# Two of the four low quarters of one weight slab moved from VectorE to GpSimd

## The chip, the cores and the metric

The kernel runs on one core of a Trainium2 chip. The metric is the device time of one execution in microseconds; the figure for a kernel is the median of its runs. The engines are PE (TensorE), DVE (VectorE), ACT (ScalarE), POOL (GpSimd) and SP (SyncE, which issues the loads).

## The reference, cut to what matters

One decoder layer on 512 tokens of width 1024, all in float32. The stretch that the change touches is the combined input projection and, inside it, the index scores of the sparse attention:

```python
h = _rmsnorm(x, norm_mix[l])
proj = h @ w_in[l]
(q_sb, k_sb, v_sb, q_sa, k_sa, v_sa, q_ix, k_ix, w_ix, g_sb, g_sa) = _split_cols(proj)
q_sa = _rmsnorm(q_sa.reshape(B, S, SA_HEADS, HEAD_DIM), q_norm_sa[l])
...
# per block of 128 queries (IDX_HEADS = 8 index heads of width 32)
rel = jnp.einsum('bthd,bsd->bths', qib, k_idx) * (Di ** -0.5)
score = jnp.einsum('bth,bths->bts', wb, jax.nn.relu(rel))
score = jnp.where(key_pos[None, None, :] <= qpos[None, :, None], score, -jnp.inf)
_, idx = lax.top_k(score, top_k)        # top_k = 128 keys per query
```

Behind it stand two attentions (stick-breaking and the sparse one over the chosen keys), two gated branch projections, an output projection and a squared-ReLU MLP.

## The kernel before, in words

**Weights in two parts.** TensorE multiplies in a rounded float32 format, so each float32 operand is split into a high part (a rounded copy) and a low part (the value minus its high part), and a product is three matmuls: high by high, high by low, low by high. Weights come in slabs of 128 x 2048: SP loads a slab into one of four buffers `raw`, ACT copies it rounded into `cut_hi` (`act_cut`, L412, counts `hi_done`), DVE subtracts (`dve_cut`, L420) and writes `cut_lo`. The counter `lo_done` goes up by one for each slab that is finished, in slab order; PE waits for it before it uses a slab (`slab_ready`), and SP waits for it before it loads over the same `raw` buffer.

**The projection groups.** Five groups of 512 columns, two slabs each: KVI, QSB, KSB (group 2), QSA (group 3), VSB. Slab 6 is the first half of QSA, the sparse query slab, and slab 7 the second half. For each group PE runs two halves of four token tiles `m`, twelve matmuls each. While PE projects KSB, it also makes the index logits: after every third matmul it issues one index matmul (L1732), numbered u = 0 to 23: token block b = u // 8 + 1, head u % 8. The last token block (b = 3, 512 keys wide) has u = 16 to 23.

**The index loop.** Logit u goes to one of two PSUM banks, ACT takes its ReLU into one of two buffers `rel` (L796), and DVE multiplies by the head's weight and adds into `topmask[b]` (L1185 for the first head, L1188 for the others). Two buffers on each step make a ring:

```python
if u >= 2:
    pe.wait_ge(relu_done, u - 1)        # PE: logit u waits for ReLU u-2
...
if u >= 2:
    act.wait_ge(score_done, u - 1)      # ACT: ReLU u waits for score u-2
...
dve.wait_ge(relu_done, u + 1)           # DVE: score u waits for ReLU u
```

Between the first four scores of the last block (u = 16 to 19), DVE makes the low part of slab 6 in four quarters of 128 x 512, one behind each score. ACT made its high quarters earlier, during u = 12 to 15.

**Around it on DVE and POOL.** For each 128-token tile of a projected group, DVE sums squares (`head_sums`, L1154), POOL makes the inverse root (L607, L608, `hr_done`), and DVE scales the tile (`head_scaled`, L1174), which frees the PSUM bank for PE's next group (`proj_out`). In group KSB, POOL's order is: causal mask and root of tile 0, causal mask and root of tile 1, root of tile 2, causal mask and root of tile 3. The order on each engine is the order in which the program is written.

Of the kernel before, what the change touches and what calls it, by code (L numbers as in the profile page):

```python
# [18 lines left out]
ALU = mybir.AluOpType  # L19
ACT = mybir.ActivationFunctionType  # L20
AX = mybir.AxisListType
F32 = mybir.dt.float32
# [5 lines left out]
S = 512  # L28
# [19 lines left out]
RAW, CUT, SLAB = 4, 2, 2048  # L48
# [3 lines left out]
KVI, QSB, KSB, QSA, VSB = range(5)  # L52
# [29 lines left out]
def block_kernel(nc, x, norm_mix, w_in, q_norm_sb, k_norm_sb, q_norm_sa, k_norm_sa,  # L82
                 w_branch_sb, w_branch_sa, w_out, norm_mlp, w_ff1, w_ff2, out):
    ctx = ExitStack()
    with ctx:
        def sb(name, shape, dt, where=ctx):
            return where.enter_context(nc.sbuf_tensor(name, shape, dt))

        def sem(name):
            return ctx.enter_context(nc.semaphore(name))  # L90
# [21 lines left out]
        cut_hi = sb("cut_hi", [P, CUT, SLAB], F32R)  # L112
        cut_lo = sb("cut_lo", [P, CUT, SLAB], F32R)
# [4 lines left out]
        raw = sb("raw", [P, RAW, SLAB], F32)  # L118
# [134 lines left out]
        hi_done = sem("hi_done")  # L253
        lo_done = sem("lo_done")
# [9 lines left out]
        gain_t = sem("gain_t")  # L264
        gain_ready = sem("gain_ready")
        kw_hi_done = sem("kw_hi_done")
        kw_cut = sem("kw_cut")
        row_sq = sem("row_sq")
        half_sq = sem("half_sq")
# [130 lines left out]
        def cut_slot(i, part, k, nk):  # L400

            w = SLAB // nk
            return part[:, i % CUT, k * w:(k + 1) * w]
# [12 lines left out]
        def dve_cut(i, part=0, parts=1):  # L416

            nc.vector.wait_ge(hi_done, i + 1)
            w = SLAB // parts
            cut = nc.vector.tensor_tensor(cut_slot(i, cut_lo, part, parts), raw[:, i % RAW, part * w:(part + 1) * w],  # L420
                                          cut_slot(i, cut_hi, part, parts).bitcast(F32), ALU.subtract)
            if part == parts - 1:
                cut.then_inc(lo_done, 1)

        def stationary_weights(i, k, nk, col, dst, rhs_hi, rhs_lo, start, stop):

            w_hi = cut_slot(i, cut_hi, k, nk)[:, col:col + P]
            w_lo = cut_slot(i, cut_lo, k, nk)[:, col:col + P]
            nc.tensor.matmul(dst, w_hi, rhs_hi, start=start, stop=False)  # L429
            nc.tensor.matmul(dst, w_hi, rhs_lo, start=False, stop=False)  # L430
            return nc.tensor.matmul(dst, w_lo, rhs_hi, start=False, stop=stop)  # L431
# [126 lines left out]
        def _(pool):  # L558
            count = [0]

            def link(ins):

                count[0] += 1
                ins.then_inc(pool_self, 1)
                pool.wait_ge(pool_self, count[0])
# [30 lines left out]
            for g in range(4):  # L596
                nh = 2 if g == KVI else 8
                for m in range(TB):
                    if g == KSB and m != 2:
                        b = (1, 2, None, 3)[m]  # L600
                        pool.wait_ge(score_done, 8 * b)
                        diag = topmask[b][:, b * P:(b + 1) * P]
                        pool.affine_select(out=diag, in_=diag, compare_op=ALU.is_ge, fill=MASKED, base=0,
                                           pattern=[[-1, P]], channel_multiplier=1).then_inc(causal_done, 1)
                    pool.wait_ge(ss_done, n_norm + 1)
                    j = n_norm % 2
                    link(pool.tensor_scalar(head_ms[:, j, 0:nh], head_ss[:, j, 0:nh], 1.0 / HD, EPS, ALU.mult, ALU.add))  # L607
                    pool.tensor_tensor(head_r[:, j, 0:nh], head_ms[:, j, 0:nh], minus_half[:, 0:nh],  # L608
                                       ALU.pow).then_inc(hr_done, 1)
                    n_norm += 1  # L610
                if g == QSB:

                    link(pool.iota(dist_i, pattern=[[-1, S]], base=S - P, channel_multiplier=1))
                    pool.tensor_copy(dist[:, :], dist_i).then_inc(dist_done, 1)
                    link(pool.memset(topmask[0], 0.0))
                    pool.affine_select(out=topmask[0], in_=topmask[0], compare_op=ALU.is_ge, fill=MASKED, base=0,
                                       pattern=[[-1, P]], channel_multiplier=1).then_inc(mask0, 1)
# [78 lines left out]
            for v, q in enumerate((S4, A22)):  # L696
                m, n = PART[q]
                for t in range(2):
                    pool.wait_ge(drained, prod_end(FG - 1, S3 if (q, t) == (A22, 1) else S2) - 1 + t)
                    part = xres[:, m + t, n * 512:(n + 1) * 512]  # L700
# [366 lines left out]
        def _(dve):  # L1067
# [110 lines left out]
            def index_scores(part, cut=None):  # L1178

                for u in range(4 * part, 4 * part + 4):  # L1180
                    b, h = u // 8 + 1, u % 8
                    dve.wait_ge(relu_done, u + 1)
                    src, wgt = rel[u % 2][:, 0:(b + 1) * P], w_tok[:, b, h:h + 1]
                    if h == 0:
                        V.tensor_scalar(topmask[b], src, wgt, None, ALU.mult).then_inc(score_done, 1)  # L1185
                    else:
                        dve.wait_ge(score_done, u)
                        V.scalar_tensor_tensor(out=topmask[b], in0=src, scalar=wgt, in1=topmask[b],  # L1188
                                               op0=ALU.mult, op1=ALU.add).then_inc(score_done, 1)
                    if cut is not None:  # L1190
                        dve_cut(cut, u % 4, 4)

            for g in range(5):
                if g == KVI:
                    head_sums(0)
                    head_scaled(0)
                    head_sums(1)
                    head_scaled(1)
                    head_sums(2)
                if g == QSB:  # L1200
                    for m in range(TB):
                        dve.wait_ge(qix_hi, m + 1)
                        t = slice(m * P, (m + 1) * P)
                        V.tensor_tensor(q_parts[1][:, :, t], bank(4 + m % 2, P, 3 * P).rearrange("p (a b) -> p a b", a=2),
                                        q_parts[0][:, :, t].bitcast(F32), ALU.subtract).then_inc(tr_out, 1)
                        if m == 1:
                            dve_cut(2 * KVI + 3)
                if g == KSB:
                    dve.wait_ge(w_ready, 1)
                    index_scores(0, 2 * QSB + 3)  # L1210
                    index_scores(1)
                if g == KVI:
                    dve_half(2)
                    dve_cut(2, 1, 2)
                elif g != KSB:
                    dve_cut(2 * g + 2)
                if g < 4:
                    if g == KVI:
                        dve.wait_ge(kix_low, 1)
                        link(V.tensor_tensor(kw_sb[0:40, :], bank(6)[0:40, :], kw_low[0:40, :], ALU.add))  # L1220
                        link(V.tensor_copy(k_parts[0][0:IXD, :], kw_sb[0:IXD, :]))
                        V.tensor_tensor(k_parts[1][0:IXD, :], kw_sb[0:IXD, :], k_parts[0][0:IXD, :].bitcast(F32),
                                        ALU.subtract).then_inc(kix_out, 1)
                    if g == KSB:
                        for m in range(TB):
                            index_scores(2 + m, 2 * g + 2 if m == 2 else None)
                            if m < 3:
                                head_sums(4 * g + m)
                            if m in (1, 2):
                                head_scaled(4 * g + m - 1)  # L1230
                    for m in range(2 if g in (KVI, KSB) else 0, TB):
                        if g in (QSB, QSA) or m == 3:
                            head_sums(4 * g + m)
                        if g == QSB and m == 3:
                            dve.wait_ge(ix_stacked, 20 * 16)
                            V.tensor_copy(k_stack[:, :], k_in)
                            V.tensor_copy(q_stack[:, 4:8, :], q_in[:, 4:8, :]).then_inc(ix_ready, 1)
                        if g >= KSB:
                            topk(2 if g == QSA else 1)
                        head_scaled(4 * g + m)  # L1240
                else:
                    for m in range(TB):
                        dve.wait_ge(proj_done, 16 + m + 1)
                        V.tensor_copy(v_sb[:, m, :], bank(proj_bank(VSB, m))).then_inc(proj_out, 1)
                        topk((1, 1, 4, 0)[m])
                if g in (KSB, QSA):
                    dve_cut(2 * g + 3)
                if g in (KSB, QSA):
                    topk(4)
# [806 lines left out]
```

## Time and profile before

| what | us |
|---|---|
| runs before | 725.20, 725.34, 723.14 (median 725.2) |
| the profiled execution | 725.06 |
| its span in the trace | 723.2 |
| PE busy in the span | 715.8 (99%) |
| DVE busy | 536.8 (74%) |
| ACT busy | 341.3 (47%) |
| POOL busy | 261.5 (36%) |

The time outside the span is 725.06 - 723.2 = 1.9 us. The granted TensorE clock has a mean of 0.999 over the span. A timeline row gives the start, the duration, the engine, the line, the operation, and what is written from what; a note in brackets tells how long the engine was idle before and who released it. The records of matmuls overlap, so a wait on PE is best seen as a longer distance between starts.

### The profile page before, as it was taken

The numbers are of one execution on the slowest core, as the hardware profiler recorded it, in microseconds if no ns is written. First come the engines' busy times: TensorE is split into PE (matmuls) and PEld (weight loads), VectorE is DVE, ScalarE is ACT, GpSimd is POOL, SyncE is SP. The second block draws the span as 40 slices with busy tenths as digits, with TensorE's granted clock in tenths as the row PEclk, the third lists the DMA queues.
The fourth block names the chain that finished last, engine by engine and source line by source line (L and its number), as shares of the span: only waits on it lengthen the run. The fifth ranks groups of instructions, "written<-read, shape, count | busy, mean of one in ns | idle before, by whom it ended". The sixth has DMA issues, their size and how long they took to land.

```text
span 723.2 us, 9771 instructions
## 1 busy us (share of the span) xinstructions
PE 715.8 (99%) x3454; PEld 574.7 (79%) x3454; DVE 536.8 (74%) x771; ACT 341.3 (47%) x492; POOL 261.5 (36%) x207
## 2 busy tenths in 40 slices
PE   8999999999999999999999999999999999999997
PEld 5878878787777676788889978888888888888886
DVE  7355889899886876537746569695968779595897
ACT  6244753365567787722334353634344252634341
POOL 2005225011224563003300091815336180815586
PEclk9999999999999999999999999999999999999999
DMA  9309231311110301133290225151331505131103
GB/s 332 142 15 258 92 117 58 117 59 59 59 59 10 109 21 39 59 117 117 67 310 14 83 80 176 59 174 59 117 115 48 184 0 175 57 116 58 59 1 117
DMA packets 44039, 70.65 MB, mean 98 GB/s; under 512 B 2657, under 2 KB 27489, under 8 KB 44002
## 3 DMA queue, kind: packets, MB, share of 16 engines
q1 hardware_dynamic: 44000, 70.16, 29.4%
q8 instruction: 22, 0.36, 0.2%
q14 instruction: 15, 0.12, 0.1%
q10 hardware_dynamic: 2, 0.00, 0.0%
HBM read 65.71 MB, written 2.10 MB: 94 GB/s over the span
## 4 chain that ended last, share of the span: by engine, by line
PE 95%; DVE 2%; ACT 1%; POOL 1%; issue 1%; DMA 0%; DVEq 0%; ACTq 0%
PE ps L1950 8%; PE ps L1951 8%; PE ps L1952 8%; PE ps L1979 7%; PE ps L1980 7%; PE ps L1981 7%; PE ps L436 7%; PE ps L438 6%; PE ps L437 6%; PE ps L429 6%; PE ps L431 6%; PE ps L430 6%; PE ps L1861 1%; PE ps L1871 1%; PE ps L1755 1%; PE ps L1789 1%
## 5 line engine op out<-in xcount | busy, mean ns | idle before, releaser
L1950 PE MATMUL ps<-b_hi,cut_hi 128*128 128x512 f32 (+1 forms) x280 | 104.0, 371 | 0.0
L1951 PE MATMUL ps<-b_lo,cut_hi 128*128 128x512 f32 (+1 forms) x280 | 103.8, 371 | 0.0
L1952 PE MATMUL ps<-b_hi,cut_lo 128*128 128x512 f32 (+1 forms) x280 | 103.8, 371 | 0.0
L653 POOL TENSOR_TENSOR a_lo<-qo_sb,a_hi 128x512 fp32r<-128x512 f32 x56 | 93.9, 1700 | 14.2 <-ACT a_hi L976 14.2
L436 PE MATMUL ps<-cut_hi,a_hi 128*128 128x512 f32 x216 | 86.4, 400 | 0.0
L438 PE MATMUL ps<-cut_hi,a_lo 128*128 128x512 f32 x216 | 84.5, 391 | 0.0
L437 PE MATMUL ps<-cut_lo,a_hi 128*128 128x512 f32 x216 | 84.3, 390 | 0.0
L965 ACT ACTIVATE qo_sb<-ps 128x512 f32<-128x512 f32 x32 | 19.2, 599 | 130.2 <-PE ps L1952 84.0
L420 DVE TENSOR_TENSOR cut_lo<-raw,cut_hi 128x2048 fp32r<-128x2048 f32 (+2 forms) x33 | 51.2, 1551 | 28.0 <-ACT cut_hi L412 28.0
L661 POOL TENSOR_TENSOR qo_sb<-qo_sb 128x512 f32<-128x512 f32 x7 | 9.1, 1293 | 151.8 <-DVE qo_sb L1409 151.8
L412 ACT ACTIVATE cut_hi<-raw 128x2048 fp32r<-128x2048 f32 (+2 forms) x33 | 48.5, 1469 | 31.2 <-PE ps L431 22.7
L1952 PEld LDWEIGHTS ps<-b_hi,cut_lo 128*128 128x128 f32 x280 | 52.8, 188 | 9.1
L1950 PEld LDWEIGHTS ps<-b_hi,cut_hi 128*128 128x128 f32 x280 | 52.7, 188 | 9.0
L1951 PEld LDWEIGHTS ps<-b_lo,cut_hi 128*128 128x128 f32 x280 | 52.8, 188 | 8.9
L1481 DVE TENSOR_TENSOR gates<-ps,gates 128x512 f32<-128x512 f32 x80 | 51.4, 676 | 5.9 <-PE ps L1981 5.2
L1979 PE MATMUL ps<-cut_hi,a_hi 128*128 128x512 f32 (+1 forms) x142 | 54.9, 387 | 0.1
L1981 PE MATMUL ps<-cut_hi,a_lo 128*128 128x512 f32 (+1 forms) x142 | 54.8, 386 | 0.0
L1980 PE MATMUL ps<-cut_lo,a_hi 128*128 128x512 f32 (+1 forms) x142 | 54.8, 386 | 0.0
L429 PE MATMUL ps<-a_hi,cut_hi 128*128 128x512 f32 x128 | 54.5, 425 | 0.0
L431 PE MATMUL ps<-a_hi,cut_lo 128*128 128x512 f32 x128 | 50.3, 393 | 0.0
L430 PE MATMUL ps<-a_lo,cut_hi 128*128 128x512 f32 x128 | 50.1, 391 | 0.0
L1409 DVE SCALAR_TENSOR_TENSOR qo_sb<-ps,qo_sb 128x512 f32<-128x512 f32 x32 | 21.9, 685 | 36.1 <-ACT qo_sb L965 36.1
(218 smaller groups left out, 1650.4 us busy)
## 6 DMA issues: line engine op xcount, KB each, us to landing
raw<-in_w_ff_dram SPq DMA_DIRECT2D x32, 1024.0 KB, 5.5
raw<-in_w_in_dram SPq DMA_DIRECT2D x16, 1024.0 KB, 5.4
gates<-in_x_dram SPq DMA_DIRECT2D x8, 512.0 KB, 5.7
raw<-in_w_out_dram SPq DMA_DIRECT2D x4, 1024.0 KB, 5.1
raw<-in_w_in_dram SPq DMA_DIRECT2D x4, 512.0 KB, 7.1
raw<-in_w_branch_sb_dram SPq DMA_DIRECT2D x2, 1024.0 KB, 5.1
raw<-in_w_branch_sa_dram SPq DMA_DIRECT2D x4, 512.0 KB, 6.3
out_dram<-gates SPq DMA_DIRECT2D x7, 256.0 KB, 2.8
```

Source lines behind the costliest of these rows:

```text
L429: nc.tensor.matmul(dst, w_hi, rhs_hi, start=start, stop=False)
L431: return nc.tensor.matmul(dst, w_lo, rhs_hi, start=False, stop=stop)
L436: nc.tensor.matmul(dst, l_hi, w_hi, start=start, stop=False)
L437: nc.tensor.matmul(dst, l_hi, w_lo, start=False, stop=False)
L438: return nc.tensor.matmul(dst, l_lo, w_hi, start=False, stop=stop)
L653: return pool.tensor_tensor(left_lo[:, q], left[q], left_hi[:, q].bitcast(F32), ALU.subtract).then_inc(l_lo, 1)
L1950: T.matmul(dst, w_hi[:, w], b_hi[:, k, a:b], start=(k == 0), stop=False)
L1951: T.matmul(dst, w_hi[:, w], b_lo[:, k, a:b], start=False, stop=False)
L1952: mm = T.matmul(dst, w_lo[:, w], b_hi[:, k, a:b], start=False, stop=(k == KD - 1))
L1979: T.matmul(dst, l_h, hi[:, j, a:b], start=(opens or a > 0) and j == 0, stop=False, skip_group_check=True)
L1980: T.matmul(dst, l_h, lo[:, j, a:b], start=False, stop=False, skip_group_check=True)
L1981: mm = T.matmul(dst, l_l, hi[:, j, a:b], start=False, stop=(j == 1), skip_group_check=True)
```

## The change

POOL gets quarters 2 and 3 of the low part of slab 6 (`i = 2 * KSB + 2 = 6`). It makes them after the root of KSB's tile 1 and ahead of the root of tile 2, and its second one raises `lo_done`. DVE keeps quarters 0 and 1, behind the scores u = 16 and u = 17, and counts them in a new semaphore `quarter_lo`; POOL waits for two of these before its quarter 3, so that `lo_done` means the whole slab. DVE waits for `lo_done` to stand at 7 before it makes slab 7, so that the counter rises in slab order.

```diff
+        quarter_lo = sem("quarter_lo")
...
             if part == parts - 1:
                 cut.then_inc(lo_done, 1)
+            return cut
...
                     pool.tensor_tensor(head_r[:, j, 0:nh], head_ms[:, j, 0:nh], minus_half[:, 0:nh],
                                        ALU.pow).then_inc(hr_done, 1)
                     n_norm += 1
+                    if g == KSB and m == 1:
+                        i = 2 * KSB + 2
+                        pool.wait_ge(hi_done, i + 1)
+                        pool.wait_ge(lo_done, i)
+                        for part in (2, 3):
+                            if part == 3:
+                                pool.wait_ge(quarter_lo, 2)
+                            lo = pool.tensor_tensor(cut_slot(i, cut_lo, part, 4), raw[:, i % RAW, part * S:(part + 1) * S],
+                                                    cut_slot(i, cut_hi, part, 4).bitcast(F32), ALU.subtract)
+                        lo.then_inc(lo_done, 1)
...
-                    if cut is not None:
+                    if cut == 2 * KSB + 2 and u % 4 < 2:
+                        dve_cut(cut, u % 4, 4).then_inc(quarter_lo, 1)
+                    elif cut is not None and cut != 2 * KSB + 2:
                         dve_cut(cut, u % 4, 4)
...
                 if g in (KSB, QSA):
+                    if g == KSB:
+                        dve.wait_ge(lo_done, 2 * KSB + 3)
                     dve_cut(2 * g + 3)
```

On DVE, at the scores u = 16 to 23 (`topm` is `topmask`, `lg` holds the ReLU buffers), stood before:

```order
L1185 TENSOR_SCALAR topm<-lg,w_tok 128x512
L420 TENSOR_TENSOR cut_lo<-raw,cut_hi 128x512
L1188 SCALAR_TENSOR_TENSOR topm<-lg,w_tok,topm 128x512
L420 TENSOR_TENSOR cut_lo<-raw,cut_hi 128x512
L1188 SCALAR_TENSOR_TENSOR topm<-lg,w_tok,topm 128x512
L420 TENSOR_TENSOR cut_lo<-raw,cut_hi 128x512
L1188 SCALAR_TENSOR_TENSOR topm<-lg,w_tok,topm 128x512
L420 TENSOR_TENSOR cut_lo<-raw,cut_hi 128x512
L1154 TENSOR_REDUCE head_ss<-gates 128x8
L1174 TENSOR_TENSOR gates<-ps,head_r 128x512
```

and stands now (the lines are numbered by the new file; L421 is the subtract, L1200 the score):

```order
L1197 TENSOR_SCALAR topm<-lg,w_tok 128x512
L421 TENSOR_TENSOR cut_lo<-raw,cut_hi 128x512
L1200 SCALAR_TENSOR_TENSOR topm<-lg,w_tok,topm 128x512
L421 TENSOR_TENSOR cut_lo<-raw,cut_hi 128x512
L1200 SCALAR_TENSOR_TENSOR topm<-lg,w_tok,topm 128x512 x2
L1166 TENSOR_REDUCE head_ss<-gates 128x8
L1186 TENSOR_TENSOR gates<-ps,head_r 128x512
```

The scores u = 18 and u = 19 now follow each other, and the subtract behind each of them is gone.

On POOL, from the causal mask of tile 1 to the root of tile 2, stood before:

```order
L603 AFFINE_SELECT topm<-topm 128x128
L607 TENSOR_SCALAR head_ms<-head_ss 128x8
L608 TENSOR_TENSOR head_r<-head_ms,minus_half 128x8
L607 TENSOR_SCALAR head_ms<-head_ss 128x8
L608 TENSOR_TENSOR head_r<-head_ms,minus_half 128x8
```

and stands now:

```order
L605 AFFINE_SELECT topm<-topm 128x128
L609 TENSOR_SCALAR head_ms<-head_ss 128x8
L610 TENSOR_TENSOR head_r<-head_ms,minus_half 128x8
L620 TENSOR_TENSOR cut_lo<-raw,cut_hi 128x512 x2
L609 TENSOR_SCALAR head_ms<-head_ss 128x8
L610 TENSOR_TENSOR head_r<-head_ms,minus_half 128x8
```

Two subtractions of 128 x 512 moved in between the roots of tiles 1 and 2. PE, ACT and SP issue what they issued before, in the same order.

## Rows read from the trace of the kernel before

**Rows 1.** The page's head: span, then busy time by engine.

```profile
span 723.2 us, 9771 instructions
PE 715.8 (99%) x3454; PEld 574.7 (79%) x3454; DVE 536.8 (74%) x771; ACT 341.3 (47%) x492; POOL 261.5 (36%) x207
```

**Rows 2.** Timeline of PE, 87.7 to 92.7 us (start, duration, engine, line).

```profile
87.70 0.39 PE L1732 MATMUL ps<-k_stack,q_stack 128*128 128x512 f32 x1
...
88.61 0.39 PE L1732 MATMUL ps<-k_stack,q_stack 128*128 128x512 f32 x1
...
89.76 0.50 PE L1732 MATMUL ps<-k_stack,q_stack 128*128 128x512 f32 x1
...
91.03 0.50 PE L1732 MATMUL ps<-k_stack,q_stack 128*128 128x512 f32 x1
...
92.30 0.50 PE L1732 MATMUL ps<-k_stack,q_stack 128*128 128x512 f32 x1
92.63 0.40 PE L436 MATMUL ps<-cut_hi,a_hi 128*128 128x512 f32 x1
```

**Rows 3.** The chain that ended last, 90 to 92 us (start, duration, what).

```profile
90.81 0.76 DVE topm L1188
91.65 0.61 ACT lg L796
```

**Rows 4.** Timeline of DVE, 88 to 92 us, and the four scores behind.

```profile
88.28 0.74 DVE L1188 SCALAR_TENSOR_TENSOR topm<-lg,w_tok,topm 128x512 f32<-128x512 f32 x1
88.94 0.68 DVE L420 TENSOR_TENSOR cut_lo<-raw,cut_hi 128x512 fp32r<-128x512 f32 x1
89.54 0.74 DVE L1188 SCALAR_TENSOR_TENSOR topm<-lg,w_tok,topm 128x512 f32<-128x512 f32 x1
90.20 0.69 DVE L420 TENSOR_TENSOR cut_lo<-raw,cut_hi 128x512 fp32r<-128x512 f32 x1
90.81 0.75 DVE L1188 SCALAR_TENSOR_TENSOR topm<-lg,w_tok,topm 128x512 f32<-128x512 f32 x1
91.47 0.69 DVE L420 TENSOR_TENSOR cut_lo<-raw,cut_hi 128x512 fp32r<-128x512 f32 x1
...
93.26 3.31 DVE L1188 SCALAR_TENSOR_TENSOR topm<-lg,w_tok,topm 128x512 f32<-128x512 f32 x4
```

**Rows 5.** Timeline of ACT, the ReLU of u = 20.

```profile
90.38 0.60 ACT L796 ACTIVATE lg<-ps 128x512 f32<-128x512 f32 x1 [0.18 <-DVE topm L1188]
```

**Rows 6.** Timeline of POOL, the root of tile 1.

```profile
87.14 1.64 POOL L608 TENSOR_TENSOR head_r<-head_ms,minus_half 128x8 f32<-128x8 f32 x1
```

**Rows 7.** Timeline of POOL in the MLP, subtractions alone and under DVE's.

```profile
416.50 1.30 POOL L653 TENSOR_TENSOR a_lo<-qo_sb,a_hi 128x512 fp32r<-128x512 f32 x1
...
425.51 10.39 POOL L653 TENSOR_TENSOR a_lo<-qo_sb,a_hi 128x512 fp32r<-128x512 f32 x5
```

**Rows 8.** Timeline of DVE, 428 to 435 us, under the five of [rows 7].

```profile
428.01 1.21 DVE L1416 TENSOR_TENSOR cut_lo<-qT_sa,cut_hi 128x1024 fp32r<-128x1024 f32 x1
429.14 2.31 DVE L1447 TENSOR_TENSOR qT_sa<-raw,qT_sa 128x1024 f32<-128x1024 f32 x1
431.38 3.38 DVE L1365 TENSOR_TENSOR cut_lo<-raw,cut_hi 128x2048 fp32r<-128x2048 f32 x1
```

**Rows 9.** Timeline of DVE and POOL at 82 us, scores against POOL.

```profile
81.50 0.62 DVE L1188 SCALAR_TENSOR_TENSOR topm<-lg,w_tok,topm 128x384 f32<-128x384 f32 x1 [0.25 <-ACT lg L796]
...
82.63 1.37 DVE L1188 SCALAR_TENSOR_TENSOR topm<-lg,w_tok,topm 128x384 f32<-128x384 f32 x2
...
82.81 0.49 POOL L607 TENSOR_SCALAR head_ms<-head_ss 128x8 f32<-128x8 f32 x1 [4.07 <-DVE head_ss L1154]
...
86.86 0.20 POOL L607 TENSOR_SCALAR head_ms<-head_ss 128x8 f32<-128x8 f32 x1 [0.72 <-DVE head_ss L1154]
```

**Rows 10.** Timeline of DVE and PE, 100 to 103 us: tile 3's bank.

```profile
100.89 0.69 DVE L1174 TENSOR_TENSOR gates<-ps,head_r 128x512 f32<-128x512 f32 x1 [1.28 <-POOL head_r L608]
...
102.16 0.48 PE L436 MATMUL ps<-cut_hi,a_hi 128*128 128x512 f32 x1
```

## The prediction

> **What bounds the kernel now.** I read the page's busy times first, then the chain that ended last, then the timelines of the engines in the one stretch where that chain leaves PE. PE is busy for 715.8 of 723.2 us [rows 1], so a change elsewhere counts only where PE waits for it. The chain runs along PE nearly throughout, but at 88 to 92 us it runs over DVE and ACT [rows 3]: the score u = 19 on DVE, the ReLU of u = 21, and from there PE's last index matmul. The distance between the starts of PE's index matmuls shows the wait: u = 19 and u = 20 start at 87.70 and 88.61, 0.91 apart, which is a step of four matmuls without a wait; the next start at 89.76, 91.03 and 92.30, 1.15, 1.27 and 1.27 apart [rows 2]. So PE loses 0.24 + 0.36 + 0.36 = 0.96 us here, and no more than that can be won.
>
> The pace is DVE's: a score and a quarter take 1.27 us (88.28 to 89.54, 89.54 to 90.81) [rows 4], of which the quarter is 0.61 (90.20 to 90.81). The ring passes it on: the ReLU of u = 20 starts at 90.38, right behind score 18 (89.54 + 0.74 = 90.28) [rows 4, 5], and PE's logit 22 at 91.03 right behind that ReLU (90.38 + 0.60 = 90.98) [rows 2, 5]. In the same way score 19 ends at 91.56, ReLU 21 runs from 91.65 to 92.26, and logit 23 starts at 92.30 [rows 2 to 4]. Hence **logit 22 moves with the end of score 18, and logit 23 with the end of score 19**. Behind logit 23 PE has no score to wait for in this group, and its next work is the slab in question, at 92.63 [rows 2].
>
> **The change part by part.**
>
> *What DVE is relieved of.* Two quarters go. But the first of them stands behind score 18 and the second behind score 19. Logits 21 and 22 wait for scores 17 and 18, which have the same instructions ahead of them as before. Only score 19 has one quarter less ahead: -0.61 us on its end, and of that only 0.36 us is a wait of PE. The quarter behind score 19 (91.47) delays only scores 20 to 23, for which no PE work in this group waits. So the largest gain is 0.36 us, at the last logit.
>
> *What POOL adds.* POOL is free at 87.14 + 1.64 = 88.78 [rows 6]; ACT's high part of the slab has long been made by then. A 128 x 512 subtract of the same kind takes POOL 1.30 us where it has the way free [rows 7]. But POOL and DVE get in each other's way. Five such subtractions in a row take 10.39 us instead of about 5 x 1.26 [rows 7], and while they run DVE's subtractions become longer too: 2.31 us for a 128 x 1024 that takes 1.21 just ahead of it, and 3.38 for a 128 x 2048 [rows 8]. From 428.01 to 429.14 the free one takes 1.13 to the next start; the next takes 2.24 (429.14 to 431.38). So **one POOL subtract that gets in costs DVE 2.24 - 1.13 = 1.11 us**, and the rows read as turns: one DVE instruction, one POOL instruction, one DVE instruction, although DVE's stand back to back. I take 1.10 for each.
>
> *Where they meet here.* POOL's quarter 2 is ready at 88.78, while DVE is in score 17 (88.28 to 89.02) [rows 4]. DVE's quarter 1 follows at 88.94. By turns, POOL goes ahead of it, and the quarter comes out 1.10 later: score 18 starts at about 90.64 instead of 89.54 and ends at 91.38. POOL's quarter 3 waits for DVE's quarter 1 (done at 90.72), so it is ready while score 18 runs, and it gets in ahead of score 19. Score 19 could start at 91.30; with another 1.10 it ends at 91.30 + 0.66 + 1.10 + 0.10 = 93.16 instead of 91.56. POOL is done with the slab at about 92.5.
>
> *Do scores take turns with POOL as subtractions do?* This decides whether the second 1.10 falls due. A score reads two buffers in SBUF, as a subtract does. The one place in the trace where a score met POOL is at 82.63: POOL's small instruction takes 0.49 instead of 0.20, its end (83.30) falls just behind the end of the first score (82.63 + 0.62 = 83.25), and two scores together take 1.37, where each alone takes 0.62 [rows 9]. I read that as turns, on one occurrence and with a tiny POOL operand; I take the full 1.10.
>
> The Trainium skill has a rule that speaks against this change: in "SBUF — State Buffer", section "SBUF: two separate sides", VectorE and GpSimd share a port pair as an exclusive lock, which a VectorE instruction with two SBUF inputs and a GpSimd instruction that reads SBUF can't hold together, and whoever comes second blocks for the whole instruction. By that rule both the quarter and the scores pay and the sum is the one below; with scores outside the rule it would be the smaller one of the second rival. The rows on subtractions agree with it at 1.11 us per turn; for scores the trace has the one small row.
>
> *The sum.* Logit 22: +1.10 (92.13 instead of 91.03). Logit 23: + 2 x 1.10 - 0.61 = **+1.6 us** (93.9 instead of 92.30). This replaces the first delay, it isn't added to it: logit 23 waits for ReLU 21, whichever is later.
>
> *What is late next, and what covers it.* PE comes to slab 6 at about 94.2; POOL finished it at 92.5, so that wait costs nothing, with 1.7 us of cover. The root of tile 2 on POOL finds its sums later than POOL is done, so POOL doesn't hold it up. DVE gives back part of its delay behind score 19, since the second quarter is gone there. The next place where PE needs DVE is the bank of tile 3, scaled at 100.89 + 0.69 = 101.58 and used by PE at 102.16 [rows 10]. PE arrives 1.6 later and DVE about 0.6 to 1.2 later, so it stays covered. DVE's new wait ahead of slab 7 stands some 10 us behind POOL's signal; were POOL late there, DVE's top-k steps would queue behind it. SP's load over the freed buffer follows the same counter at about the same time (92.5 against 91.47 + 0.69 = 92.16), far ahead of its use. Behind 94 us PE runs as densely as before, so nothing takes the 1.6 us back. The profiled execution's own time is 725.06, against a median of 725.2: **725.06 + 1.6 = 726.7 us**.
>
> **The rivals.**
>
> *As meant: no meeting of the two engines.* Then score 19 is 0.61 earlier, logit 23 0.36 earlier, slab 6 done at 88.78 + 2 x 1.26 + 0.1 = 91.4, ahead of PE: 724.7. Against it stand [rows 7, 8].
>
> *Scores don't take turns, subtractions do.* Quarter 1 pays 1.10, score 18 and logit 22 with it. Quarter 3 runs beside scores 18 and 19. Score 19 ends at 92.06, so logit 23 is bound by PE's own step behind logit 22: 92.13 + 1.0 = 93.15, +0.85: 725.9. For it: the score row is weak [rows 9].
>
> *DVE keeps its turn while it has work back to back, POOL starves.* Then the scores are not late, but slab 6 is. Quarter 2 gets in at about 90.9, when score 19 is over, and ends at 92.2; quarter 3 competes with scores 20 to 23, which run 1.3 us earlier than the 93.26 to 96.57 of before [rows 4]. If it gets in only behind them it ends at 95.3 + 1.3 = 96.6, and PE waits there instead of going on at 92.63: +4.0, 729.1. From quarter 3 ending later than 94.8 on, this is slower by over 0.3%; if it gets in at once behind quarter 2 (93.5), it is +0.9. Against it: POOL got its turn between DVE's back-to-back subtractions [rows 7, 8].
>
> *The change does not do what it says* has no room: two subtractions are gone from DVE's list and two stand in POOL's.
>
> **How the numbers follow.** Turns for both: 0.60. Scores free: 0.20. As meant: 0.07. POOL starves: 0.08. The rest, 0.05, for something I don't see, mostly slower. The unknowns are the share of the second 1.10 and a spread of the runs of some 2 us (723.14 to 725.34). The range reaches from 724.6 (as meant) to 728.2 (turns at 1.3 each, 2 x 1.3 - 0.61 = 2.0, and the spread of the runs); most of starvation is left out. About 0.3%, or 2.2 us, is what a measurement of this kernel can tell from no change. The forecast of +1.6 is 0.22%, inside that bound but near it: I give a quarter of its 0.60 to slower (0.15), and add 0.06 of starvation and 0.03 of the rest. Slower 0.24, same 0.73, faster 0.03.
>
> **What would show each step.** Turns: DVE's quarter 1 lengthened from 0.68 to about 1.8, and score 19 from 0.75 to about 1.8, with score 18 starting near 90.6; POOL's two subtractions together ending near 92.5. If score 19 stays at 0.75, scores don't take turns. The sum: index matmuls 22 and 23 on PE near 92.1 and 93.9, the first matmul of the sparse queries near 94.2, and the rest of the span shifted by the same 1.6. I am wrong if quarter 1 keeps its 0.68 us (no meeting), if PE waits at the first matmul of slab 6 (starvation), or if a later wait swallows or doubles the shift.

## The result and the profile after

| kernel | median, us | lowest, us | ratio to before |
|---|---|---|---|
| before | 723.83 (22 runs) | 723.10 | 1 |
| changed | 724.72 (22 runs) | 724.54 | 1.0022, 95% interval 1.0014 to 1.0030 |

The change makes the kernel slower by 0.22%, which is 1.6 us on 723.83 (interval 1.0 to 2.2). This ratio lies near that of the means (725.50 and 723.97, 1.53 us apart); the medians lie only 0.89 us apart, the lowest times 1.44. The forecast was +1.6 us, 726.7 us as a time, with a range from 724.6 on. The measured median is 2 us below 726.7, just inside the range, for two reasons: the profiled execution of before, on whose 725.06 us the sum was made, lies 1.2 us above the median of its own runs (723.83), and the medians differ by 0.7 us less than 1.6. Of all executions behind the ratios in this text one, of e1_left_out, took 1974 us and is left out. The profiled execution of the changed kernel took 724.68 us with a span of 722.9.

The two spans can't be compared as they are. The first tile of the changed kernel's execution ran earlier by 0.59 us (its first matmul on the slabs at 16.80 instead of 17.39), and its span ends 1.1 us sooner behind the last matmul. So everything below goes by distances inside one trace. The measure is **the time on PE from index matmul 20 to the first matmul on slab 6**, the stretch in which PE waits for the ring. Before it was 92.63 - 88.61 = 4.02 us [rows 2]. After, the timeline of PE (start, duration, engine, line; a bracket gives the idle time before) shows:

```profile
88.01 0.39 PE L1748 MATMUL ps<-k_stack,q_stack 128*128 128x512 f32 x1
...
89.17 0.50 PE L1748 MATMUL ps<-k_stack,q_stack 128*128 128x512 f32 x1
...
91.53 0.50 PE L1748 MATMUL ps<-k_stack,q_stack 128*128 128x512 f32 x1 [1.16 <-ACT lg L808]
...
93.20 0.50 PE L1748 MATMUL ps<-k_stack,q_stack 128*128 128x512 f32 x1 [0.48 <-ACT lg L808]
93.53 0.39 PE L438 MATMUL ps<-cut_hi,a_hi 128*128 128x512 f32 x1
```

93.53 - 88.01 = 5.52 us, 1.50 more. Index matmul 21 keeps its distance (1.16 against 1.15 us), 22 comes 2.36 us behind it instead of 1.27, and 23 another 1.67 instead of 1.27. Nearly all of this lasts: slab 6 starts 0.90 us later than in the trace of before (93.53 and 92.63), and PE's last matmul still 0.82 us later (720.04 and 719.22).

DVE in the same stretch, to be held against [rows 4]:

```profile
87.68 0.74 DVE L1200 SCALAR_TENSOR_TENSOR topm<-lg,w_tok,topm 128x512 f32<-128x512 f32 x1
88.34 1.78 DVE L421 TENSOR_TENSOR cut_lo<-raw,cut_hi 128x512 fp32r<-128x512 f32 x1
90.04 2.41 DVE L1200 SCALAR_TENSOR_TENSOR topm<-lg,w_tok,topm 128x512 f32<-128x512 f32 x2
92.38 0.67 DVE L1166 TENSOR_REDUCE head_ss<-gates 128x8 f32<-128x512 f32 x1
```

Quarter 1 takes 1.78 us instead of 0.68. Scores 18 and 19, which stand as one row here, take 2.41 us together: score 18 has its 0.74, score 19 starts at 90.89 and takes 1.57 instead of 0.75. Quarter 1 and score 19 each meet a subtract of POOL:

```profile
86.54 1.64 POOL L610 TENSOR_TENSOR head_r<-head_ms,minus_half 128x8 f32<-128x8 f32 x1
88.14 1.43 POOL L620 TENSOR_TENSOR cut_lo<-raw,cut_hi 128x512 fp32r<-128x512 f32 x1
90.20 1.71 POOL L620 TENSOR_TENSOR cut_lo<-raw,cut_hi 128x512 fp32r<-128x512 f32 x1 [0.63 <-DVE cut_lo L421]
93.14 0.20 POOL L609 TENSOR_SCALAR head_ms<-head_ss 128x8 f32<-128x8 f32 x1 [1.24 <-DVE head_ss L1166]
```

POOL goes first at 88.34, score 18 goes ahead of POOL's second at 90.04, and POOL's second goes ahead of score 19. POOL finishes the slab at 91.91, PE comes to it at 93.53: that wait costs nothing.

There is a second part, which the forecast did not have. Over two sets of runs, 12 of 34 executions of the changed kernel (5 of 22 in this set, 7 of 12 in the second) took 726.8 to 728.3 us with a mean granted clock of 0.998 or less; no execution of before shows less than 0.999. The experiments come back to it.

### The profile page after: what moved, and what is told of

Read it like the earlier page. It is cut to its first block, busy times and chain, and to the rows that moved or that the text cites. A ratio compares the mean times of both kernels' runs of the same rounds, so it can differ in the third digit from the quotient of the medians.

```text
span 722.9 us, 9773 instructions
## 1 busy us (share of the span) xinstructions
PE 715.0 (99%) x3454; PEld 574.1 (79%) x3454; DVE 537.6 (74%) x769; ACT 341.2 (47%) x492; POOL 264.9 (37%) x209
## 4 chain that ended last, share of the span: by engine, by line
PE 95%; DVE 2%; ACT 1%; POOL 1%; issue 1%; DMA 0%; DVEq 0%; ACTq 0%
PE ps L1968 8%; PE ps L1966 8%; PE ps L1967 8%; PE ps L1995 7%; PE ps L1997 7%; PE ps L1996 7%; PE ps L438 7%; PE ps L440 6%; PE ps L439 6%; PE ps L431 6%; PE ps L433 6%; PE ps L432 6%; PE ps L1877 1%; PE ps L1887 1%; PE ps L1771 1%; PE ps L1805 1%
## 5 line engine op out<-in xcount | busy, mean ns | idle before, releaser
L421 DVE TENSOR_TENSOR cut_lo<-raw,cut_hi 128x2048 fp32r<-128x2048 f32 (+2 forms) x31 | 50.9, 1641 | 28.5 <-ACT cut_hi L413 28.5
```

## Experiments

The theory was the one of the prediction: POOL's and DVE's instructions take turns where both read SBUF, each turn makes the DVE instruction later, and the score ring hands that on to PE. All kernels are told by the measure above, from one trace each, and by the ratio to executions of before in the same set of runs.

| kernel | index matmul 20 to slab 6, us | ratio, 95% interval | lowest, us |
|---|---|---|---|
| before | 4.02 | 1 | 723.02 |
| changed | 5.52 | 1.0022 (1.0014 to 1.0030) | 724.54 |
| e1_left_out | 3.69 | 0.9987 (0.9977 to 0.9997) | 722.91 |
| e2_narrow | 3.95 | 0.9996 (0.9986 to 1.0005) | 723.04 |
| e3_one | 4.73 | 1.0006 (0.9997 to 1.0016) | 723.87 |
| e4_early | from matmul 19: 5.40, before 4.93 | 1.0005 (0.9995 to 1.0015) | 723.74 |
| e5_spread | 3.39 | 0.9997 (0.9987 to 1.0007) | 722.53 |
| after_again | 5.62 | 1.0030 (1.0017 to 1.0043) | 724.66 |
| e6_fill | 5.52 | 1.0012 (1.0003 to 1.0021) | 724.60 |
| e7_spread_late | 3.27 | 0.9988 (0.9980 to 0.9997) | 722.53 |

**Without POOL's subtractions.** Their work is left out, and with it the new waits; DVE keeps the new order.

```diff
-                        for part in (2, 3):
-                            ...                    # POOL's two subtractions
-                        lo.then_inc(lo_done, 1)
...
                     if cut == 2 * KSB + 2 and u % 4 < 2:
-                        dve_cut(cut, u % 4, 4).then_inc(quarter_lo, 1)
+                        low = dve_cut(cut, u % 4, 4)
+                        if u % 4 == 1:
+                            low.then_inc(lo_done, 1)
```

> The changed kernel without POOL's two subtractions: quarters 2 and 3 of the low part of slab 6 are left out (the stale low part is used), DVE's quarter 1 raises lo_done, and the new waits are gone. Measure: the time on PE from index matmul 20 to the first matmul on slab 6, which was 4.02 us before the change and is 5.52 with it. Theory of turns (a POOL subtract that gets in costs the DVE instruction behind it 1.1 us): without them score 19 comes 0.61 earlier than before, quarter 1 has 0.68 us again, and the time is 4.02 - 0.36 = 3.66, the whole kernel about 0.4 us faster than before (ratio 0.9995). Rival, that the new order on DVE costs the time (two scores in a row): it stays near 5.5, about +1.5 us.

Measured: 3.69 us (92.27 - 88.58), 0.33 less than before, against 3.66 expected; the ratio, 0.9987, came out lower than the 0.9995 expected, which its interval still holds. PE's index matmul 20 and first matmul on slab 6, then DVE's timeline:

```profile
88.58 0.41 PE L1738 MATMUL ps<-k_stack,q_stack 128*128 128x512 f32 x1
...
92.27 0.39 PE L438 MATMUL ps<-cut_hi,a_hi 128*128 128x512 f32 x1
...
88.25 0.75 DVE L1190 SCALAR_TENSOR_TENSOR topm<-lg,w_tok,topm 128x512 f32<-128x512 f32 x1
88.91 0.69 DVE L421 TENSOR_TENSOR cut_lo<-raw,cut_hi 128x512 fp32r<-128x512 f32 x1
89.51 1.60 DVE L1190 SCALAR_TENSOR_TENSOR topm<-lg,w_tok,topm 128x512 f32<-128x512 f32 x2
91.03 0.68 DVE L1156 TENSOR_REDUCE head_ss<-gates 128x8 f32<-128x512 f32 x1
```

Quarter 1 has its 0.69 us again, so the whole loss comes from POOL's subtractions or from the waits that came with them; the next run tells these apart. A side reading corrects a term: two scores in a row take 1.60, so the second starts about 1.60 - 0.74 = 0.86 behind the first, not 0.66. A score adds to what the score before it wrote and, by the program, waits for its count; with a quarter between them that wait was hidden. The trace of before had this price already: its four scores of [rows 4] take 3.31 us, which is (3.31 - 0.74) / 3 = 0.86 from one to the next.

**The same with a quarter of the width.** POOL subtracts 128 of the 512 columns; the order and all waits stay.

```diff
-   cut_slot(i, cut_lo, part, 4), raw[:, i % RAW, part * S:(part + 1) * S], cut_slot(i, cut_hi, part, 4)
+   cut_slot(i, cut_lo, part, 4)[:, 0:128], raw[:, i % RAW, part * S:part * S + 128], cut_slot(i, cut_hi, part, 4)[:, 0:128]
```

> The changed kernel with POOL's two subtractions cut to 128 of their 512 columns each (the low part of the other columns of quarters 2 and 3 is left stale); all waits and the order stay. Theory of turns: a turn costs what POOL's instruction lasts, some 0.3 us here, so score 18 is 0.3 late and score 19 on time (2 x 0.3 - 0.61), and the time from index matmul 20 to slab 6 is about 4.0 us, 0 to +0.1 on the kernel. Rival, that the handshake between the engines costs (POOL waits for DVE's quarter, DVE and PE for POOL's count): its waits are all still there, so the time stays near 5.5, +1.5 us.

Measured: 3.95 us (91.80 - 87.85), about 4.0 expected. The handshake with its waits was all there, so it isn't the cost; the length of POOL's instructions is.

```profile
88.17 0.95 DVE L421 TENSOR_TENSOR cut_lo<-raw,cut_hi 128x512 fp32r<-128x512 f32 x1
89.05 1.61 DVE L1200 SCALAR_TENSOR_TENSOR topm<-lg,w_tok,topm 128x512 f32<-128x512 f32 x2
...
87.97 0.61 POOL L620 TENSOR_TENSOR cut_lo<-raw,cut_hi 128x128 fp32r<-128x128 f32 x1
89.20 0.90 POOL L620 TENSOR_TENSOR cut_lo<-raw,cut_hi 128x128 fp32r<-128x128 f32 x1 [0.63 <-DVE cut_lo L421]
```

Quarter 1 is 0.27 longer. The two scores are not: 1.61 us against 1.60 in the run without POOL. The short second subtract costs the scores nothing that these rows can show; it has room in the 0.2 us that score 19 waits for score 18 anyway.

**One quarter on POOL.** POOL makes quarter 2 only, DVE 0, 1 and 3.

```diff
-                    if cut == 2 * KSB + 2 and u % 4 < 2:
-                        dve_cut(cut, u % 4, 4).then_inc(quarter_lo, 1)
+                    if cut == 2 * KSB + 2 and u % 4 != 2:
+                        if u % 4 == 3:
+                            dve.wait_ge(quarter_lo, 1)      # POOL's quarter 2
+                        dve_cut(cut, u % 4, 4)
```

> Half of the change: POOL makes quarter 2 alone, at its old time (88.8 us), DVE makes quarters 0, 1 and 3 behind scores 16, 17 and 19. Theory of turns: quarter 1 on DVE takes about 1.8 us, score 18 ends 1.1 later than before, score 19 by 1.10 - 0.61 = 0.49; PE's index matmul 22 comes 1.1 later and 23 about 0.86 later (one PE step of 1.03 behind 22), so index matmul 20 to slab 6 takes about 4.9 us, the kernel +0.9 (ratio 1.0012). Rival, that only the second subtract with its wait costs: quarter 1 is short, and the time is 4.02 or less, +0 us.

Measured: 4.73 us (93.59 - 88.86), 0.71 more than before, against about 0.9 expected; PE starts on slab 6 here without the restart of a wait, 0.23 us behind matmul 23 (93.36 to 93.59) instead of 0.33. The kernel's ratio does not tell +0.9 from nothing by itself. The order of turns came out otherwise than expected:

```profile
88.86 0.41 PE L1744 MATMUL ps<-k_stack,q_stack 128*128 128x512 f32 x1
...
93.59 0.39 PE L438 MATMUL ps<-cut_hi,a_hi 128*128 128x512 f32 x1
...
89.19 0.69 DVE L421 TENSOR_TENSOR cut_lo<-raw,cut_hi 128x512 fp32r<-128x512 f32 x1
89.80 2.64 DVE L1196 SCALAR_TENSOR_TENSOR topm<-lg,w_tok,topm 128x512 f32<-128x512 f32 x2
...
88.99 2.03 POOL L617 TENSOR_TENSOR cut_lo<-raw,cut_hi 128x512 fp32r<-128x512 f32 x1
```

Quarter 1 went ahead of POOL, and score 18 paid: the pair takes 2.64 against 1.60, which is 1.04 us more, and score 18 alone 1.78 instead of 0.74. Index matmul 22 comes later by the same 1.04. So a score pays as a subtract does.

**The same work earlier.** POOL makes both quarters ahead of the causal mask of tile 1; DVE's quarter 1 raises `lo_done`.

```diff
                 for m in range(TB):
+                    if g == KSB and m == 1:
+                        ...                        # POOL's two subtractions, the second one counts quarter_lo
                     if g == KSB and m != 2:
```

> The same work moved, at another time: POOL makes quarters 2 and 3 ahead of the causal mask and the root of tile 1, from about 85.6 us on, as soon as ACT's high part is there, while DVE reads PSUM or one SBUF buffer; DVE keeps quarters 0 and 1 behind scores 16 and 17. Theory of turns: POOL's second one ends near 88.1 and delays quarter 0 (87.67) by 0.4 us; behind that DVE meets no POOL subtract. Score 18 is 0.4 late, score 19 is 0.2 early; index matmul 20 to slab 6 takes 4.0 to 4.4 us, the kernel 0 to +0.4. The root of tile 1 comes 1.5 us later, which nothing needs so soon. Rival, that a subtract on POOL costs PE wherever it stands (POOL's roots late, or the port for the whole stretch): near 5.5, +1.5 us.

Measured: 5.40 us from index matmul 19 on (93.18 - 87.78), 0.47 more than before, a little over the +0.4 that was the upper end expected. The count starts at matmul 19 since the delay falls ahead of matmul 20 here, which comes 0.60 late; from 20 on it is 3.89 us. The rival's cost would give some 6.4 us from matmul 19, as in the changed kernel (93.53 - 87.11). So the size was nearly met, but not on the path expected. POOL's pair had the way free for most of its 2.55 us, while DVE read PSUM or a single buffer. But at its end it met a kind of instruction that I had taken as safe:

```profile
87.36 1.19 DVE L1195 TENSOR_SCALAR topm<-lg,w_tok 128x512 f32<-128x512 f32 x1
88.47 0.77 DVE L421 TENSOR_TENSOR cut_lo<-raw,cut_hi 128x512 fp32r<-128x512 f32 x1
...
85.72 2.55 POOL L606 TENSOR_TENSOR cut_lo<-raw,cut_hi 128x512 fp32r<-128x512 f32 x2 [0.61 <-ACT cut_hi L413]
```

Score 16 multiplies one SBUF buffer by a scalar, 0.47 to 0.48 us in all other runs, and took 1.19. So it isn't two inputs alone that make DVE take turns. The Trainium skill names such a second case: in "SBUF — State Buffer", section "SBUF: two separate sides", a VectorE instruction in a two-port performance mode contends as well. The row agrees that it waited; which mode it ran in, no row here tells.

**DVE alone, spread.** From the kernel before: DVE makes all four quarters, behind scores 14, 15, 17 and 19; a new count tells when ACT's first two high quarters are there.

```diff
+                    if u in (14, 15):
+                        i, part = 2 * KSB + 2, u - 14
+                        dve.wait_ge(quarter_hi, part + 1)
+                        V.tensor_tensor(...)       # quarter 0, quarter 1
+                    if u in (17, 19):
+                        dve_cut(2 * KSB + 2, 2 if u == 17 else 3, 4)
```

> A version without POOL, from the kernel before: DVE makes all four quarters of the low part of slab 6, but quarters 0 and 1 earlier, behind scores 14 and 15 (as soon as ACT's high quarters are there, told by a new count), quarter 2 behind score 17 and quarter 3 behind score 19. If the loss of 0.96 us on PE is set by where DVE's quarters stand in the score ring, as the chain says, and not by DVE's total work (unchanged), scores 18 and 19 end before PE's free-running logits need them: index matmul 20 to the first matmul on slab 6 takes about 3.0 to 3.2 us instead of 4.02 (5.52 with the change), and the kernel is about 0.9 us faster than before (ratio 0.9988). Rival, that the ring is bound by DVE's sum of work whatever the order: about 4.0 us and ratio 1.000.

Measured: 3.39 us (91.69 - 88.30), 0.63 less than before, but index matmul 20 itself came 0.23 late, so the net is 0.40 (4.53 from matmul 19 instead of 4.93). Less than half of the 0.9 expected, and a ratio that can't be told from 1. The rows name what was left: DVE summed and scaled tiles ahead of score 16, back to back behind the two quarters, and the chain that ended last runs there over them and score 16 to index matmul 20.

```profile
85.29 0.68 DVE L1199 TENSOR_TENSOR cut_lo<-raw,cut_hi 128x512 fp32r<-128x512 f32 x1
85.89 0.68 DVE L1158 TENSOR_REDUCE head_ss<-gates 128x8 f32<-128x512 f32 x1
86.49 0.68 DVE L1178 TENSOR_TENSOR gates<-ps,head_r 128x512 f32<-128x512 f32 x1
87.08 0.47 DVE L1189 TENSOR_SCALAR topm<-lg,w_tok 128x512 f32<-128x512 f32 x1
```

**DVE alone, spread, and the scaling behind score 19.**

```diff
                             index_scores(2 + m, 2 * g + 2 if m == 2 else None)
+                            if m == 2:
+                                head_scaled(4 * g)
                             if m < 3:
                                 head_sums(4 * g + m)
-                            if m in (1, 2):
-                                head_scaled(4 * g + m - 1)
+                            if m == 2:
+                                head_scaled(4 * g + 1)
```

> As e5_spread, and the scaling of tile 0 (0.6 us on DVE) moved from ahead of score 16 to behind score 19. In e5_spread PE still waited at index matmuls 20 and 22 since score 16 came late behind that scaling, and only about 0.4 us of the 0.96 were won. Theory (the place of DVE's work in the ring sets PE's loss): score 16 comes 0.6 us earlier, PE runs its index matmuls without a wait, index matmul 19 to the first matmul on slab 6 takes about 3.9 to 4.1 us instead of 4.93, the kernel about 0.9 us faster than before (ratio 0.9988). Rival (DVE's sum of work in the ring): about 4.5 us as in e5_spread, ratio 0.9995.

Measured: 3.27 us (91.60 - 88.33), 4.18 from matmul 19, 0.75 less than before and a little over the 3.9 to 4.1 expected; ratio 0.9988 with an interval up to 0.9997. This is below the kernel before, narrowly clear of noise, with the same work on the same engine, only placed otherwise. Index matmuls 20 to 22 now run without a wait. From matmul 23 to slab 6 it takes 0.41 us (from 91.19) instead of 0.23; the moved scaling of DVE ends just ahead of that, at 91.45, but whether it holds PE was not tested.

```profile
87.42 0.39 PE L1745 MATMUL ps<-k_stack,q_stack 128*128 128x512 f32 x1
...
88.33 0.39 PE L1745 MATMUL ps<-k_stack,q_stack 128*128 128x512 f32 x1
...
89.24 0.39 PE L1745 MATMUL ps<-k_stack,q_stack 128*128 128x512 f32 x1
...
90.14 0.50 PE L1745 MATMUL ps<-k_stack,q_stack 128*128 128x512 f32 x1
...
91.60 0.47 PE L438 MATMUL ps<-cut_hi,a_hi 128*128 128x512 f32 x1
```

**The changed kernel again.**

> The changed kernel once more, for the order of turns: in its first profile POOL's quarter 2 went ahead of DVE's quarter 1 (1.78 us instead of 0.68), with half of the change alone DVE's quarter 1 went ahead of POOL. If who goes first is a matter of a few ns, this may come out either way; by the turns the end of score 18 is 1.0 to 1.1 us late in both cases, so index matmul 20 to slab 6 stays between 5.3 and 5.6 us, and the kernel at +1.5 us (ratio 1.002). Rival: if the order decides the cost, the time differs by 0.5 us or more where the order differs.

Measured: 5.62 us (94.08 - 88.46), at the upper end of what was expected. This time DVE's quarter 1 went first (0.68 us), and POOL's two subtractions came in behind it (3.71 us together), scores 18 and 19 taking 3.45. Against 1.60 that is 1.85 us, score 18 paying as in e3_one (1.04) and score 19 as in the first profile (0.81). The order of turns thus comes out either way in one and the same kernel, and index matmul 23 comes 5.12 us behind matmul 20, against 5.19 in the first profile: it costs nothing. The rest of the 5.62 is something else, which shows in the stretches of this run (length, then busy time of each engine, granted clock, DMA):

```profile
88.00:92.00 4.00, 2.83 (x12) 1.63 (x10) 3.90 (x5) 1.98 (x4) 4.00 (x3) 1.00 0.00 0
92.00:93.60 1.60, 1.12 (x5) 0.60 (x5) 1.60 (x3) 0.60 (x1) 0.37 (x2) 1.00 0.22 19
93.60:97.00 3.40, 3.40 (x8) 2.69 (x9) 3.09 (x5) 1.96 (x4) 1.75 (x2) 0.52 0.91 300
97.00:98.00 1.00, 1.00 (x5) 0.78 (x4) 0.97 (x4) 1.00 (x1) 0.29 (x1) 0.94 0.00 0
```

Behind PE's two gaps (1.10 and 0.48 us idle by its rows) the granted clock stands at 0.52 over 3.4 us, that is at 1.2 instead of 2.4 GHz nearly throughout, and the matmuls there start 0.43 us apart instead of 0.23:

```profile
94.08 0.63 PE L438 MATMUL ps<-cut_hi,a_hi 128*128 128x512 f32 x1
94.51 0.63 PE L439 MATMUL ps<-cut_lo,a_hi 128*128 128x512 f32 x1
...
97.56 0.40 PE L438 MATMUL ps<-cut_hi,a_hi 128*128 128x512 f32 x1
97.80 0.39 PE L439 MATMUL ps<-cut_lo,a_hi 128*128 128x512 f32 x1
```

Eight matmuls at 0.20 us more (93.58 to 97.07) are 1.6 us, on top of the ring's 1.5; the expectation of the next run counts twelve matmuls, the rows show eight. In the first profile of the changed kernel the clock stayed at 1.00 behind gaps of the same size.

**The gaps on PE filled.** The changed kernel with seven spare matmuls into an unused bank.

```diff
             def index_logits(u):
+                if u in (22, 23):
+                    pe.wait_ge(tr_out, 8)
+                    for _ in range(5 if u == 22 else 2):
+                        T.matmul(bank(4), ident_b, cold_b[:, :], start=True, stop=True)
```

> The changed kernel with seven spare matmuls (128x128 by 128x512 into an unused bank) on PE in its two gaps: five ahead of index matmul 22, two ahead of index matmul 23, sized to end before the ReLU that PE waits for. Nothing else changes. In the second profile of the changed kernel the granted clock is 0.50 from about 93.6 to 97.0 us, right behind the two gaps of 1.10 and 0.48 us, and the next twelve matmuls run at half rate; its slow group of executions (about 727 us and above, 12 of 34) shows a mean clock of 0.998 or less, which no execution of the kernel before or of e1 to e5 has. Theory that the gaps on PE bring the clock down: with the gaps filled no execution is above about 726.5 us or below a mean clock of 0.999, the lowest stay at 724.5 (the score ring still sets index matmul 20 to slab 6 at 5.4 to 5.6 us), ratio 1.002. Rival, that the clock drop has another cause (the load of POOL and DVE together): about a third of the executions stay at 727 us and above.

Measured: 5.52 us (93.36 - 87.84), as in the changed kernel, so the ring is untouched. All 11 executions lie between 724.60 and 725.58 us with a mean clock of 1.000; none is at 727 us. The ratio is 1.0012, where the changed kernel had 1.0022 and 1.0030; the intervals overlap.

```profile
90.03 1.25 PE L1749 MATMUL ps<-cold_b,const_b 128*128 128x512 bf16 x5
91.35 0.50 PE L1752 MATMUL ps<-k_stack,q_stack 128*128 128x512 f32 x1
```

This speaks for PE's standing still as the cause, since DVE and POOL do the same in both, but it does not show it. The changed kernel was not run in the same set as this one, and its share of low-clock executions differed between its two sets: at 12 of 34 none in 11 would be a chance of under 1%, at the 5 of 22 of its first set one of 6%.

## Why the prediction was right, point by point

- **Logit 22 moves with the end of score 18, by one turn of 1.10 us.** Right. From matmul 20 to 22 it is 3.52 us after and 2.42 before, +1.10; quarter 1 is 1.10 longer.
- **Scores take turns too.** Right: scores 18 and 19 take 2.41 against 1.60 without POOL, and in e3_one the pair pays 1.04 us for a single subtract. The rival with free scores (+0.85) falls. But the row that the prediction rested on did not show it. It read the two scores of 128 x 384 in 1.37 us [rows 9] as a turn. Scores of 128 x 256 stand in a row in the same trace while POOL is idle (73.26 to 78.44 us):

```profile
75.06 0.47 DVE L1188 SCALAR_TENSOR_TENSOR topm<-lg,w_tok,topm 128x256 f32<-128x256 f32 x1
75.45 0.68 DVE L420 TENSOR_TENSOR cut_lo<-raw,cut_hi 128x512 fp32r<-128x512 f32 x1
76.06 2.24 DVE L1188 SCALAR_TENSOR_TENSOR topm<-lg,w_tok,topm 128x256 f32<-128x256 f32 x4
```

From one to the next these take (2.24 - 0.47) / 3 = 0.59 us, where a quarter starts 0.39 behind a score (75.06 to 75.45). The same 0.2 us explains the 1.37: 81.50 to 82.04 is 0.54 without that wait, and 0.54 + 0.2 + 0.62 = 1.36. So the row shows that POOL waited (0.49 instead of 0.20), and not that a score did. As far as this row goes, that scores pay was right by luck.

- **The sum of +1.6 for logit 23.** The measured +1.50 is close, but two of its terms were off and offset each other, which is luck. The relief was put at 0.61, the quarter alone; it is 1.27 - 0.86 = 0.41, since a score right behind a score waits for the other's result. The second turn was put at 1.10; it is 2.41 - 1.60 = 0.81. The likely reason is that the first 0.2 us of POOL's instruction fall into that same wait, where e2_narrow's short subtract fits whole and costs nothing. 1.10 + 0.81 - 0.41 = 1.50.
- **The cover of slab 6 and what comes later.** Right: POOL is done at 91.91, PE comes at 93.53, 1.6 us of cover (1.7 expected). Starvation of POOL did not happen: it got in behind one DVE instruction each time.
- **The strict order of turns.** Too strict. In the same kernel once POOL and once DVE went first at quarter 1. The cost on PE did not depend on it (5.19 and 5.12 us from matmul 20 to 23).
- **Nothing behind 94 us.** Here a step was missing. I read the two longer waits on PE as time lost once. In a third of the executions the mean clock is lower, and the one of these that was profiled loses about 1.6 us more behind the two waits. This part is in the measured ratio: without the 5 low-clock executions of the first set the means lie 1.01 us apart and not 1.53. That 0.22% met the forecast to a tenth of a microsecond is therefore luck in part. The ring's own +1.5 stands on the distances in the traces and on the lowest times, 1.44 us apart.
- **What a measurement can tell.** The prediction put it at about 0.3%. With 22 executions on each side 0.22% is clear of 1 (1.0014 to 1.0030).

## What to carry to other kernels

Elementwise work moved from VectorE to GpSimd did not relieve VectorE here, since the two read SBUF side by side in that stretch. Look at what VectorE does while GpSimd would run, and count the length of each GpSimd instruction that gets in ahead of a VectorE instruction (here 1.0 to 1.1 us, and 0.8 where VectorE would have waited anyway). In a ring of buffers ask which link the removed instruction stands ahead of: only one of the two removed here stood ahead of a score that PE waited for, and moving VectorE's own pieces to other steps of the ring won 0.12% (0.03 to 0.20%) where the second engine lost 0.22%. Where one score adds to another's result, look for the wait between them before reading a long pair as a collision. One execution lost about as much to a fallen clock behind the waits as to the added waits themselves, so read the granted clock in more than one execution.

## What had not been expected of the hardware

- The granted clock fell from 1.00 to 0.52 over 3.4 us in the profile of one execution of the changed kernel, behind gaps of 1.10 and 0.48 us on PE, and not in another with gaps of 1.16 and 0.48 us; with the gaps filled, the mean clock was 1.000 in all 11. In e3_one, which has a gap of 1.10 us and no second one, it was 0.999 or more in all 10. What decides between two executions alike stays open.
- A one-input score of 512 columns took 1.19 us instead of 0.48 under a GpSimd subtract (e4_early), while a reduction of one SBUF buffer and a scaling out of PSUM kept their 0.69 and 0.68 us beside it.
- Which of the two engines goes first, when both wait for score 17 to end, is not fixed: quarter 1 took 1.78 us in one profile of the changed kernel and 0.68 in the other.
